# Prompt attention in falling order, split exponentials, and expert sums read straight from PSUM, in a one-core decoder layer

## What is computed

```python
# differential attention, 4 heads, two score maps (m = 0, 1) per head, width 64 + 64; values 128 wide
s = einsum('bqhmd,bkhmd->bmhqk', q, k) * 64**-0.5        # + bias by distance, masked behind the diagonal
p = softmax(s, axis=-1)
w = p[:, 0] - lam * p[:, 1]
o = einsum('bhqk,bkhd->bqhd', w, v)                       # prompt: 8 query tiles; sample: 4096 paged keys
...
x  = layer_norm(alpha * x + gate1 * (concat(o_norm, o_conv) @ w_out))
h2 = x * (1 + scale2) + shift2
# expert stage: per token 8 heads x 16 experts, each a row u|v of 2 x 1024 numbers
a = gelu(einsum('thkd,td->thk', peer_u[e], h2))
f = einsum('thk,thkd->td', g * a, peer_v[e])
x = layer_norm(alpha * x + gate2 * f)
new_conv_*                                                # last two rows of the convolution, stored as they are
```

## Time and profile before

| what | value |
|---|---|
| median of 3 runs | 4059.37 us (4057.34 to 4062.81) |
| the profiled execution's own time | 4067.12 us |
| its span, first to last instruction | 4065.3 us |
| mean granted TensorE clock | 0.958 |
| busy: PE, DVE, ACT, POOL | 80%, 61%, 30%, 37% of the span |
| attention | about 533 to 1127 us of the span |
| output projection and first layer norm | about 1128 to 1303 us |
| expert stage | about 1303 to 4065 us |

### The profile page before, as it was taken

One profiled execution on the slowest core, in us unless ns is written; L12 is line 12 of the kernel. 1 busy time (PEld: TensorE's weight loads), 2 busy tenths in 40 slices (PEclk: granted clock), 3 DMA queues, 4 the chain that ended last, 5 costly groups with the idle time before them and its releaser, 6 DMA issues.

```text
span 4065.3 us, 42925 instructions
## 1 busy us (share of the span) xinstructions
PE 3256.8 (80%) x12846; PEld 1549.1 (38%) x12846; DVE 2495.9 (61%) x6184; ACT 1201.1 (30%) x3462; POOL 1515.0 (37%) x1336
## 2 busy tenths in 40 slices
PE   8799978887476788888788888888887888878876
PEld 6444646555232333333333333333333333333322
DVE  2110256554246777776776677777677767668975
ACT  2110035444100233332332233333233333233332
POOL 0000005444300344444444445444544444444343
PEclk9899989999688899999999999999999999999999
DMA  9412059888833999999999999999999999999997
GB/s 381 178 38 54 16 172 314 276 263 225 101 140 111 383 422 421 421 421 421 415 418 414 418 413 419 413 412 421 417 412 418 415 416 411 421 416 410 414 416 314
DMA packets 290771, 1359.62 MB, mean 334 GB/s; under 512 B 47536, under 2 KB 68865, under 8 KB 155384
## 3 DMA queue, kind: packets, MB, share of 16 engines
q0 software_dynamic: 172592, 1174.62, 72.3%
q1 hardware_dynamic: 84416, 136.67, 10.3%
q10 hardware_dynamic: 33544, 45.73, 3.2%
HBM read 1327.55 MB, written 29.35 MB: 334 GB/s over the span
## 4 chain that ended last, share of the span: by engine, by line
DMA 39%; PE 16%; DVE 6%; issue 2%; POOL 2%; ACT 2%; ACTq 0%; POOLq 0%; DVEq 0%
DMA sb_ring<-in_uv,sb_experts 39%; PE psum L1590 14%; DVE sb_ring L1786 4%; POOL sb_ring L1553 2%; PE psum L1577 2%; ACT sb_diag L1650 1%; ACT sb_expert_w L1644 1%; ACT sb_gelu L1641 0%; DMA sb_iota<-in_const_iota 0%; DVE sb_eab L1709 0%; DVE sb_hot L1707 0%; DVE sb_si L1694 0%; DVE sb_f L1815 0%; DVE sb_hot L1703 0%; DVE sb_f L1812 0%
## 5 line engine op out<-in xcount | busy, mean ns | idle before, releaser
L1590 PE MATMUL psum<-sb_ring,sb_diag 128*128 128x512 f32 x4224 | 1973.3, 612 | 515.8 <-ACT sb_diag L1650 515.7
L1553 POOL DMA_INDIRECT sb_ring<-in_uv,sb_experts x1056 | 1258.2, 1191 | 1511.4 <-PE psum L1590 1249.8
L1786 DVE CUSTOM_DVE_ANT_0 sb_ring<-sb_ring,sb_h 128x1024 f32<-128x1024 f32 x1056 | 1290.2, 1226 | 674.0 <-DMA sb_ring<-in_uv,sb_experts 640.4
L1590 PEld LDWEIGHTS psum<-sb_ring,sb_diag 128*128 128x128 f32 x4224 | 784.3, 193 | 1679.7 <-ACT sb_diag L1650 851.1
L1641 ACT ACTIVATE sb_gelu<-sb_dots 128x2 f32<-128x2 f32 x528 | 107.4, 203 | 1784.3 <-DVE sb_dots L1786 1784.3
L842 POOL DMA_INDIRECT sb_v_pages<-in_cache_v,sb_v_row_of x256 | 245.6, 959 | 338.0 <-PE psum L869 270.3
L1650 ACT ACTIVATE sb_diag<-sb_ident,sb_expert_w 128x128 f32<-128x128 f32 x1024 | 355.2, 394 | 16.7
L1577 PE MATMUL psum<-sb_merged_pq,sb_h2T 128*128 128x512 f32 x576 | 271.7, 596 | 11.9 <-ACTq L90 11.9
L1644 ACT ACTIVATE sb_expert_w<-sb_gelu,sb_gates 128x1 f32<-128x1 f32 x1056 | 253.3, 287 | 17.3
L834 POOL IOTA sb_lane<- 128x1 int32 x1 | 0.1, 118 | 533.7 <-POOLq L113 533.7
L445 PE MATMUL psum<-sb_w_qkv,sb_hT_tile 128*128 128x512 f32 (+1 forms) x432 | 189.1, 598 | 0.0
(11 more groups left out here) (213 smaller groups left out, 2527.0 us busy)
## 6 DMA issues: line engine op xcount, KB each, us to landing
sb_k_pages<-in_cache_k SPq DMA_DIRECT2D x256, 256.0 KB
sb_w_ada<-in_w_ada SPq DMA_DIRECT2D x12, 2048.0 KB
sb_ring<-in_uv,sb_experts POOLq DMA_INDIRECT x1056, 16.8
sb_w_pq<-in_w_pq ACTq DMA_DIRECT2D x4, 2048.0 KB, 27.3
merged_scratch<-sb_merged ACTq DMA_DIRECT2D x8, 1024.0 KB, 13.3
sb_merged_pq<-merged_scratch SPq DMA_DIRECT2D x4, 2048.0 KB, 22.6
sb_w_qkv<-in_w_in ACTq DMA_DIRECT2D x3, 2048.0 KB
sb_w_bcu<-in_w_in SPq DMA_DIRECT2D x12, 512.0 KB, 6.4
```

The source lines that it names most:

```text
L1553: pool.indirect_dma_start(ring[:, slot, :], None, uv, bass.IndirectOffsetOnAxis(ap=e_all[:, t, k + s:k + s + 1], axis=0))\
L1590: ins = nc.tensor.matmul(psum[:, 2 * (t % 2) + n, :], diag[:, q % CHAINS, s, :], ring[:, slot, D + n * BANK:D + (n + 1) * BANK], start=(k ...
L1786: nc.vector.tensor_tensor_reduce(ring[:, slot, 0:D], ring[:, slot, 0:D], h[:, t % 2, :], 1.0, 0.0, ALU.mult, ALU.add, dots[:, q % CHAINS, ...
```

## The change

Four things change in the order and the shape of the work; what is computed stays. First, prompt tiles go in falling order: units of 8 blocks come first, from step 0, and those of 1 block last, from step 110 to 116. Wide units begin every four or six steps in turn (0, 4, 10, 14, 20, then 26 to 78), narrow ones every two (84, then 86 to 116), never before the transposes of the unit that used their place in `scores`. Second, a wide unit's two exponentials stand in two steps, the mix one step later, and transposes two steps behind the mix. Third, the last sample's chunks are drawn together: one per step instead of one per two, with both value halves in one step, so STEPS falls from 151 to 144. Fourth, in the expert stage DVE multiplies the sums straight from PSUM with the gate, and ACT's copy is gone; the other pieces stand at other pairs. The statistics `row_max`, `neg_max` and `row_sum` get eight places instead of four.

```diff
+    def tile_of(k):
+        return TILES - 1 - k // H
+
     def keys_of(k):
-        return (k // H + 1) * P
+        return (tile_of(k) + 1) * P
...
+    def e_before(k):
+
+        if keys_of(k) > BANK:
+            return k - 2
+        return k - 4 if k - 4 >= UNITS // 2 else UNITS // 2 - 2 + (k % 4) // 2
...
     for g in range(CHUNKS):
         b, c = g // NCH, g % NCH
         MAXES[2 * g + 4] = g
-        EXPS[sample_step(b) + 19 + 2 * c] = g
-        TURN[sample_step(b) + 20 + 2 * c] = g
-        TURNED[sample_step(b) + 21 + 2 * c] = g
...
-    ENDS = {sample_step(b) + 37: b for b in range(NB)}
-    STEPS = sample_step(NB - 1) + 38
+        at = sample_step(b) + 19 + (2 * c if b < NB - 1 else c + min(c, 1))
+        EXPS[at], TURN[at + 1], TURNED[at + 2] = g, g, g
+        for i in range(2):
+            VALUES.setdefault(at + 3 + (i if b < NB - 1 and c < NCH - 1 else 0), []).append(2 * g + i)
+        if c == NCH - 1:
+            ENDS[at + 4] = b
+    NEW_TURN, NEW_TURNED, NEW_VALUES = ({sample_step(b) + at: b for b in range(NB)} for at in (21, 22, 23))
+    STEPS = max(ENDS) + 1
...
-    taken = set(NEW_TURN)
+    taken = set(NEW_TURN) | {at for at in TURN if at % 2}
+    at, turned_at = 0, []
     for k in range(UNITS):
-        at = 2 * (k * 16 // 10) if k < UNITS // 2 else 50 + 6 * (k - UNITS // 2)
+        two = len(parts_of(k)) == 2
+        if e_before(k) >= 0:
+            at = max(at, (turned_at[e_before(k)] + 1) // 2 * 2)
         for c in range(len(parts_of(k))):
             P_SCORES[at + c] = (k, c)
             P_MAXES[at + c + 1] = (k, c)
-        at += len(parts_of(k))
-        P_EXPS[at + 1] = k
-        P_MIXED[at + 2] = k
-        turn = at + 3
+        for m in range(2):
+            P_EXPS.setdefault(at + (3 + m if two else 2), []).append((k, m))
+        mixed = at + (5 if two else 3)
+        P_MIXED[mixed] = k
+        turn = mixed + 2
...
+        turned_at.append(turn)
         if k % H == H - 1:
-            P_OUT[turn + 2] = k // H
+            P_OUT[turn + 3] = tile_of(k)
+        at += 2 if not two else 6 if k % 2 else 4
...
-                def prompt_exps(k):
+                def prompt_exps(k, m):
                     act.wait_ge(T["p_ready"], k + 1)
-                    for m in range(2):
-                        s = e_part(k, m, 0, keys_of(k))
-                        step(nc.scalar.activation(s, s, ACT.Exp, bias=pnmx[:, k % 4, m:m + 1], accum_out=pz[:, k % 4, m:m + 1]))
-                    step.tell(T["p_exp"])
+                    s = e_part(k, m, 0, keys_of(k))
+                    step(nc.scalar.activation(s, s, ACT.Exp, bias=pnmx[:, k % 8, m:m + 1], accum_out=pz[:, k % 8, m:m + 1]))
+                    if m:
+                        step.tell(T["p_exp"])
...
-                def collected(t):
-                    act.wait_ge(T["freed"], last_of(t) + 1)
-                    if t:
-                        act.wait_ge(T["y_stored"], 16 * t)
-                    step(nc.scalar.copy(f[:], flat(psum[:, 2 * (t % 2):2 * (t % 2) + 2, :])))
-                    step.tell(T["f_free"], T["f_ready"])
...
                 def finish(t, n):
                     if n == 0:
-                        dve.wait_ge(T["f_ready"], t + 1)
+                        dve.wait_ge(T["freed"], last_of(t) + 1)
+                        if t:
+                            dve.wait_ge(T["y_stored"], 16 * t)
+                        sums = flat(psum[:, 2 * (t % 2):2 * (t % 2) + 2, :])
+                        step(nc.vector.tensor_tensor(f[:], sums, gate2[:, t // TILES], ALU.mult))
+                        step.tell(T["f_free"])
                     elif n == 1:
-                        step(nc.vector.tensor_tensor(f[:], f[:], gate2[:, t // TILES], ALU.mult))
-                        step.done()
-                    elif n == 2:
                         dve.wait_ge(T["xres_land"], 16 * (t + 1))
...
-                FINISH = {8: 0, 9: 1, 10: 2, 11: 3, 14: 4, 15: 5, 16: 6}
+                AFTER = [(7, 9, 11, 15, 17, 19)] * (TILES - 1) + [(7, 8, 9, 12, 13, 14)]
```

More of the change, by code:

```diff
@@ L927, in prompt_values @@
                     k, c = BATCHES[n]
-                    t, h = k // H, k % H
+                    t, h = tile_of(k), k % H
                     a, width = parts_of(k)[c]
                     pe.wait_ge(T["w_copied"], n + 1)
-                    if h == 0 and c == 0 and t:
-                        pe.wait_ge(T["o_copied"], t)
+                    if h == 0 and c == 0 and k:
+                        pe.wait_ge(T["o_copied"], k // H)
                     for i in range(width // P):
@@ L1050, in _ @@
                         exps(EXPS[s])
-                    if s in P_EXPS:
-                        prompt_exps(P_EXPS[s])
+                    for k, m in P_EXPS.get(s, ()):
+                        prompt_exps(k, m)
                     if s in P_OUT:
@@ L1170, in biased @@
                         if c:
-                            step(nc.vector.tensor_tensor(pmx[:, k % 4, 0, :], pmx[:, k % 4, 0, :], pmx[:, k % 4, 1, :], ALU.max))
+                            step(nc.vector.tensor_tensor(pmx[:, k % 8, 0, :], pmx[:, k % 8, 0, :], pmx[:, k % 8, 1, :], ALU.max))
                             step.done()
-                        step(nc.vector.tensor_scalar(pnmx[:, k % 4, :], pmx[:, k % 4, 0, :], -1.0, None, ALU.mult))
+                        step(nc.vector.tensor_scalar(pnmx[:, k % 8, :], pmx[:, k % 8, 0, :], -1.0, None, ALU.mult))
                         step.tell(T["p_ready"])
@@ L1178, in mixed @@
                     dve.wait_ge(T["p_exp"], k + 1)
-                    step(nc.vector.reciprocal(prz[:], pz[:, k % 4, :]))
+                    step(nc.vector.reciprocal(prz[:], pz[:, k % 8, :]))
                     step.done()
@@ L1488, in peer @@
              ("consts h_land0 h_land1 hT_psum hT_ready sc_psum sc_free e_ready gx_ready gx_done g_ready dots_ready gelu_done wgt_done "
-              "diag_ready freed f_free f_ready xres_land xres_free var_ready sd_ready y_ready y_stored").split()}
+              "diag_ready freed f_free xres_land xres_free var_ready sd_ready y_ready y_stored").split()}
         land = [sem(f"pr_land{s}") for s in range(RING)]
@@ L1829, in _ @@
                     for t in range(TILES):
-                        if q - last_of(t) in FINISH:
-                            finish(t, FINISH[q - last_of(t)])
-                for n in range(7):
+                        if q - last_of(t) in AFTER[t]:
+                            finish(t, AFTER[t].index(q - last_of(t)))
+                for n in range(6):
                     finish(TILES, n)
```

38 lines of the change are left out of this document (11 added, 27 removed).

## The result

The changed kernel takes 4078.04 us (median of 6 runs, 4070.53 to 4083.21) against 4061.09 of the kernel before in the same runs (4057.34 to 4067.65): ratio 1.0038, 95% interval 1.0026 to 1.0051, so some 15 us slower. That lies inside the forecast range (4043 to 4080), at its slow end: the likeliest case said 4060, the slower one 4080.

What follows compares the result with a forecast made beforehand. Gathers bound the expert stage; PE's work and waits set attention's key steps, stores and page issues its tail. Key steps +4.1, step 0 +1, tail -3.5, expert end -1.2 sum to +0.4 us: 4060 in terms of the median, range 4043 to 4080.

Steps and rivals of the forecast that it cites:

- the likeliest case: Whole kernel: no measurable change, 4060 us, with a rest per plain step between 0.37 and 0.52; chance 0.48.
- The slower case: Attention key steps: the split frees nothing, rest 0.64 per plain step, +20.7 us, 4080; decides from 0.52 on; chance 0.23.
- Where it is decided: Attention's gain or loss moves everything behind it one for one; the gather-paced expert stage gives only 1.2 us at its end.
- Prompt work moved from an idle tail into full steps: Attention: 17.9 us of PE work leaves the tail, where it costs little, for key steps that PE nearly fills.
- second parts: Wide units' second part of scores in key steps: each costs PE 1.96 us waiting plus 0.92 low clock, 2.9 together.
- the prediction's prices: PE time per piece of work in attention, such as 0.97 us for key transposes and 0.645 for a prompt block.
- The split: Wide units' exponentials a step apart: removes 2.35 us of waits per unit, adds about 1.6 every second unit; rest becomes 0.45.
- plain steps: Key steps without a wait for a second part of scores; their rest is time beyond priced PE work, forecast per step.
- the second and third stretch: Key steps 21 to 50 and 51 to 85: forecast 119.8 and 132.8 us, against 96.5 and 136.7 before.
- 86 to 124: 114.0 + 39 x 0.34, narrow as in the second stretch of before: 127.3: Last key steps: 114.0 us of PE work plus 0.34 rest in each of 39 steps; 161.1 us before.
- The tail: Behind key step 124: without wide units, POOL's page issues wait less for PE, -3.5 us (bounds 0 and -6.4).
- Last sample, statistics: Attention: drawing the last sample's chunks together is worth nothing by itself; eight places for the statistics cost nothing.

Runs made afterwards that it cites:

- run 2: Changed kernel with the expert stage of the kernel before, so the attention parts alone: ratio 1.0038 to the kernel before.
- run 1: Kernel before with the expert part of the change alone: 4062.23 us against 4063.71, ratio 0.9993.
- run 9: Changed kernel with no prompt maxima or mix in steps where DVE ends a sample, and the state stored by rows: 4008.04 us, ratio 0.9874 to before.
- run 12: Kernel before with state stored by rows, wide exponentials in two steps, mix a step later and never where a sample ends: 3994.10 us, ratio 0.984.
- run 8: Changed kernel with no prompt maxima and no mix in a step where DVE ends a sample: ratio 1.0005 to the kernel before.
- run 3: Changed kernel with both exponentials of a wide unit again in one step: 4095.56 us, ratio 1.0074 to the kernel before.
- run 7: Changed kernel with the last sample's chunks two steps apart as before (151 steps): ratio 1.0036 to the kernel before.
- run 10: Kernel before with the state stored by rows: 4013.45 us, ratio 0.9884 to the kernel before.
- run 11: Changed kernel with the state stored by rows: 4021.51 us, ratio 0.9906 to the kernel before.

## Why the prediction was right and wrong

- *Where it is decided.* Right: attention has the whole loss (run 2). The end of the expert stage gave 1.17 us in the trace; the time of run 1 agrees with that and is too coarse to show it.
- *Prompt work moved from an idle tail into full steps.* Right as a cost: 17.9 us of PE work and three more waits for second parts, 2.9 each, are 26.6 us by the prediction's prices. Measured, the falling order with split and clear ends (run 9) takes 20.2 us more in the key steps than the rising order with the split (run 12): 443.6 against 423.4. It is not the whole of the loss, since what the split saves stands against it: with the meetings on DVE cleared (run 8) the key steps are only 1.8 us over those of before.
- *The split.* Right in sign and about in size: 11.8 us in run 3, where 0.72 less 0.45 a step over some 53 plain steps in the second and third stretch gives 14 (with the mix in it, which run 3 leaves out). Wrong in its place: most of it is the copy of weights, for which the probabilities' transposes wait, less the key copy.
- *The step that failed* is "86 to 124: 114.0 + 39 x 0.34, narrow as in the second stretch of before: 127.3". That stretch measured 138.8. The step put meetings of DVE's pieces at nothing beyond the average of before. The second stretch of before has one, end and mix in step 37, within its average; the late stretch of the changed kernel has three, of maxima and end, two of them with a mix. Without these three steps (22.1 us in all, 9.0 of PE work) the rest is (138.8 - 22.1 - 105.0) / 36 = 0.33 a step, the 0.34 that was taken; and run 8, which clears them, has 128.8. That the second and third stretch came near their forecasts is partly luck: there the end meets wide units' maxima, key steps 37, 53 and 69 with the next ones are 10.5 us shorter in run 8, and its two stretches lie 2.2 and 1.5 us below the forecast. The slower case came true by its number (rest 0.58 on the average, (462.5 - 353.1 - 46.4) / 108, above its 0.52) and not by its mechanism: the split did free something. That the range holds 4078 is owed to that case, so it is luck. The sums of DVE's work in each step could be added up from the tables, as ACT's were, and I had not done it.
- *The tail.* Forecast -3.5, in the traces -14.0, and -8.6 between runs 2 and 1. The prediction named a change of more than 7 as a sign that it is wrong, but executions of one schedule differ by as much (14 and 19 us), so that sign can't be read from single traces. By the medians it is 15.4 - 18.2 + 1.2 = -1.6 us (-6.4 to 3.7 by the interval of the ratio). Its size with the stores in it stays open. That idle time hides most of the wide units there follows from the medians: work and waits of 26.6 us left the tail, and it grew shorter by 6.4 at most; without the stores it grew shorter by 8.9 (runs 10 and 11).
- *Last sample, statistics.* Nothing, as said (run 7 for the first).

## What to carry to other kernels

Where steps are woven by a table, add up each in-order engine's work step by step, not only that of the engine that waits: three steps in which two or three harmless pieces met on DVE cost 9.7 us (22.1 against 12.3 in run 8), nearly what the split had gained, and changing their order inside the step gained 1.8 there and lost more elsewhere. Before work is moved out of a stretch that looks idle or late, ask what makes it so: here it was 18 small stores, worth three times the whole change, and the idle time that they made was a cheap place for the wide units.

## What the runs showed of the hardware

- A store of 512 single numbers among page loads lengthened the key steps by 3.8 us (68.5 us for 18). From 4 to 10 us behind each of them the core moved 21 to 143 GB/s, against 170 to 371 in the 6 us ahead, at DMA shares of 0.14 to 0.96. 8 stores of rows had no cost that could be measured.
- Executions of one schedule differ in the tail with the small stores: 131.2 and 145.2 us in executions of 4067.12 and 4080.65, 117.2 and 136.6 in executions of 4073.13 and 4092.01. That the stores alone set the spread from run to run is not shown: without them 5 runs of run 12 lie within 3.2 us and 4 of run 9 within 2.9, but 4 of run 11 within 10.7, where 9 of before on the same chip lie within 11.6.
- Behind PE's waits of 2.02 and 1.35 us in one step, eight transposes that take 1.04 to 1.06 us took 1.92, and the groups ahead of and behind them 1.09 for 0.66 and 1.08 for 0.64: 1.8 us on top of 3.4 of waiting. The granted clock was 0.50, the lower level (1.2 GHz), from 939.50 to 944.10 us, and 1.00 in the 2 us from 936.00 and from 946.00 on.
